# Mixing stage of a two-layer hybrid trunk: next pair's decay products and powers placed between this pair's corner products

## What is computed

```python
w_pre = rwkv_w0 + tanh(wl) @ rwkv_w2                    # decay product
decay = exp(-exp(-softplus(-w_pre) - 0.5))
a = sigmoid(rwkv_a0 + al @ rwkv_a2)
g = sigmoid(gl) @ rwkv_g2
kk = k * k_k; kk = kk * rsqrt(sum(kk * kk) + 1e-12)     # key norm
k_d = k * (1 + (a - 1) * k_a); b_d = kk * a
# scan over time, two directions:
S = S * w + (S @ -kk) b_d^T + v k_d^T ;  y = S r
bonus = sum(sum(r * k_d * r_k) * v)
```

## Time and profile before

| | before |
|---|---|
| median of 3 runs | 2956.99 us (2953.68 to 2960.45) |
| the profiled execution | 2950.64 us, span 2948.9 us |
| PE busy | 2860.9 us (97% of the span) |
| PEld, DVE, ACT busy | 58%, 43%, 25% |
| mean granted TensorE clock | 0.994 |
| mixing of layer 1, pairs | about 100 to 785 us of the span |
| mixing of layer 2, pairs | about 1860 to 2432 us of the span |

### The profile page before, as it was taken

One profiled execution on the slowest core, in us unless ns is written; L12 is line 12 of the kernel. 1 busy time (PEld: TensorE's weight loads), 2 busy tenths in 40 slices (PEclk: granted clock), 3 DMA queues, 4 the chain that ended last, 5 costly groups with the idle time before them and its releaser, 6 DMA issues.

```text
span 2948.9 us, 57155 instructions
## 1 busy us (share of the span) xinstructions
PE 2860.9 (97%) x25177; PEld 1721.3 (58%) x25177; DVE 1260.5 (43%) x2571; ACT 724.0 (25%) x1453; POOL 48.3 (2%) x76
## 2 busy tenths in 40 slices
PE   7999999999999999999999999999999999999999
PEld 3555555555654554444444444666666677788887
DVE  2566656555322221133333211566666643323551
ACT  3233333322222221011111001344333322211110
POOL 1000000000000000010000000000000000000000
PEclk9999999999999999999999999999999999999999
DMA  7111111111243333244444324212111124344554
GB/s 253 51 43 40 40 47 40 34 43 44 76 114 100 99 102 99 75 114 120 137 130 136 87 79 122 76 48 57 50 53 47 52 49 135 105 129 135 151 151 120
DMA packets 499989, 264.24 MB, mean 90 GB/s; under 512 B 42864, under 2 KB 493888, under 8 KB 499232
## 3 DMA queue, kind: packets, MB, share of 16 engines
q1 hardware_dynamic: 498016, 251.57, 29.9%
q0 software_dynamic: 1728, 9.03, 0.9%
HBM read 255.31 MB, written 5.24 MB: 88 GB/s over the span
## 4 chain that ended last, share of the span: by engine, by line
PE 90%; ACT 4%; DVE 4%; issue 1%; POOL 0%; DMA 0%; POOLq 0%; DVEq 0%; ACTq 0%
PE psum L453 56%; PE psum L1068 8%; PE psum L474 2%; PE psum L676 2%; PE psum L514 1%; PE psum L899 1%; PE psum L887 1%; ACT arena L1488 1%; PE psum L877 1%; PE psum L744 1%; PE psum L779 1%; PE psum L793 1%; PE psum L829 1%; PE psum L762 1%; PE psum L666 1%
## 5 line engine op out<-in xcount | busy, mean ns | idle before, releaser
L453 PE MATMUL psum<-hT,strips 128*128 128x512 f32 (+1 forms) x3968 | 1449.5, 512 | 4.0 <-ACT arena L1496 2.1
L453 PEld LDWEIGHTS psum<-hT,strips 128*128 128x128 f32 x3968 | 726.1, 190 | 504.2 <-issue 433.9
L1068 PE MATMUL psum<-arena,strips 128*128 128x512 f32 (+1 forms) x704 | 227.6, 486 | 0.6 <-DVE arena L2313 0.6
L1068 PEld LDWEIGHTS psum<-arena,strips 128*128 128x128 f32 x704 | 133.7, 190 | 93.5 <-issue 83.5
L453 PE MATMUL psum<-arena,strips 128*128 128x512 f32 (+1 forms) x512 | 167.9, 486 | 2.0 <-DVE done L2193 2.0
L1812 DVE TENSOR_SCALAR arena<-arena 128x512 f32<-128x512 f32 (+1 forms) x88 | 37.0, 420 | 278.9 <-ACT arena L1669 278.8
L1669 ACT COPY arena<-psum 128x512 f32<-128x512 f32 (+1 forms) x88 | 42.2, 480 | 412.2 <-PE psum L453 397.4
L453 PEld LDWEIGHTS psum<-arena,strips 128*128 128x128 f32 x512 | 97.1, 190 | 69.9 <-issue 60.7
L2159 DVE SCALAR_TENSOR_TENSOR arena<-arena,psum 128x512 f32<-128x512 f32 (+1 forms) x32 | 17.7, 554 | 268.1 <-PE psum L453 268.1
L2313 DVE SCALAR_TENSOR_TENSOR arena<-psum,mod,arena 128x256 f32<-128x256 f32 x24 | 10.9, 481 | 194.3 <-PE psum L1068 194.3
L1971 DVE TENSOR_TENSOR arena<-psum,tables 128x1024 f32<-128x1024 f32 x48 | 58.5, 1218 | 77.6 <-PE psum L676 77.6
(11 more groups left out here) (247 smaller groups left out, 3216.0 us busy)
## 6 DMA issues: line engine op xcount, KB each, us to landing
strips<-in_w_in_dram SPq DMA_DIRECT2D x158, 512.0 KB, 4.0
strips<-in_ffn_up_dram SPq DMA_DIRECT2D x88, 512.0 KB, 4.3
strips<-in_ada_w_dram SPq DMA_DIRECT2D x80, 512.0 KB, 4.1
strips<-in_ffn_down_dram SPq DMA_DIRECT2D x32, 512.0 KB, 4.0
arena<-in_ada_w_dram SPq DMA_DIRECT2D x4, 2048.0 KB, 14.6
strips<-in_w_in_dram SPq DMA_DIRECT2D x32, 256.0 KB, 3.8
strips<-in_a_out_w_dram SPq DMA_DIRECT2D x16, 512.0 KB, 4.1
strips<-in_rwkv_out_w_dram SPq DMA_DIRECT2D x16, 512.0 KB, 4.1
```

What stands on the lines that cost most here:

```text
L453: ins = mm(s.o[:, first:T], strip[:, b, k, :], rhs[:, k, first:T], k == 0, k == KT - 1)
L1068: ins = mm(s.o[:, lo:T], strip[:, b, j, :], hid[:, k, lo:T], k == 0, k == FT - 1)
```

## The change

The same work is done; its order inside the pair loop of `mix` changes on three engines, and two numbers of fill.

- PE: the bonus sums move from behind `corner_below` to behind the pair products `s10`, ahead of the corners. The second corner (`tr`) leaves `corners` and stands as `corners_right` behind `below_left`, just ahead of the value products. The next pair's two decay products move up: the first behind the pair products `s11`, the second ahead of `below_left`; the gate input `g` stays. The fill behind it becomes 2 units instead of 4 in layer 2, and `hop` there 2.15 instead of 2.
- ACT: the tanhs follow the copy of the first corner; the powers stand between the centre tap of k, the copy of `t10` and the key norm; the table loads move, one behind `head_inverse`, one ahead of the powers. Each tanh group now also waits for the bonus slot of this pair to be filled.
- DVE: `bonus` moves ahead of the mask of `s11`; `decays` and the first scan stand ahead of the copies of `x10`, the second scan behind them; four steps of the next pair's hats stand ahead of the chain over the chunks.

```diff
 # PE, pair loop
                     half_step(i)
                     pair_products(1, 0, i)
+                    bonus_sums(i)
                     fill(steps, 10 if wide or not ahead else 4)
                     corners(i)
                     pair_products(1, 1, i)
+                    if ahead:
+                        decay(0, i + 1)
                     fill(steps, 6 if wide or not ahead else 4)
+                    if ahead:
+                        decay(1, i + 1)
                     below_left(i)
+                    corners_right(i)
                     value_products(i)
                     fill(steps, 4 if wide or not ahead else 3)
                     corner_below(i)
-                    bonus_sums(i)
                     fill(steps, 4 if wide or not ahead else 5)
                     if ahead:
                         key_sums(i + 1)
-                        decays(i + 1)
-                        fill(steps, 4)
+                        gate_in(i + 1)
+                        fill(steps, 4 if wide else 2)
                     through_inverse(i, ahead)
-                    hop = (3.7 if ahead else 4) if wide else 2 if ahead else 2.3
+                    hop = (3.7 if ahead else 4) if wide else 2.15 if ahead else 2.3
 # ACT
+                def decay(q, i):
+                    if i > 0:
+                        act.wait_ge(*slots["bonus", l, i - 1].full)
+                    s = filled(f"decay{q}", i)
 ...
                     if i > 0:
                         head_inverse(i - 1)
+                        if ahead:
+                            exps_and_tanhs()
                     corners(i)
+                    if ahead:
+                        decay(0, i + 1)
+                        decay(1, i + 1)
+                    corners_right(i)
                     value_products(i)
                     if ahead:
                         centre(1, "k", i + 1, 0)
+                        logs()
+                        powers(0, i + 1)
                     else:
                         keys(1)
                     corner_below(i)
                     if ahead:
+                        powers(1, i + 1)
                         if lo:
                             conv_gate(i + 1)
                         key_norm(i + 1)
-                        decays(i + 1)
+                        gate_in(i + 1)
                     through_inverse(i)
                     if ahead:
                         if lo == 0:
                             conv_gate(i + 1)
-                        powers(0, i + 1)
-                        powers(1, i + 1)
 # DVE
+                    bonus(i)
                     masked_pairs(1, 1, i)
+                    if ahead:
+                        decays(i + 1)
+                        sums(0)
                     below_left(i)
                     if ahead:
+                        sums(1)
                         s = taps(1, "k", i + 1, 0, 1)
                         key_squares(i + 1, s)
-                    bonus(i)
                     state_in(0, i)
-                    if ahead:
-                        decays(i + 1)
                     steps = hats(i + 1) if ahead else iter(())
+                    for _ in range(EARLY_HATS):
+                        next(steps, None)
```

More of the change, by code:

```diff
@@ L621, in key_sums, with gate_in @@
                     one(s.o, tab["heads"], rinv_k).then_inc(s.full[0], 1)
[L623 to L629, removed]
+                def decay(q, i):
+                    if q == 0:
+                        pe.wait_ge(*lr.full())
+                    s = take(Q, f"decay{q}", l, i)
+                    for h in range(2):
+                        ins = one(PS[:, BANK_P[s.b] + h, :], lw[rows(h), q, :], low[rows(h), q, :])
+                    ins.then_inc(s.full[0], 1)
+                def gate_in(i):
                     s = take(A, "g", l, i)
@@ L705, in corners, with corners_right @@
                     ins.then_inc(s.full[0], 1)
+                def corners_right(i):
                     s = take(A, "tr", l, i)
@@ L991, in mix @@
                 pe.wait_ge(ev["low_ready"], l + 1)
-                decays(0)
+                decay(0, 0)
+                decay(1, 0)
+                gate_in(0)
                 pe.drain().then_inc(lr.free, 1)
@@ L1405, in key_norm @@
                 def key_norm(i):
-                    if i < 2:
+                    if i == 0:
                         logs()
@@ L1411, in key_norm, with decay, gate_in @@
                     act.activation(rinv_k, rinv_k, ACT.Exp, scale=-0.5).then_inc(ev["rinv_ready"], 1)
[L1412 to L1421, removed]
+                def decay(q, i):
+                    if i > 0:
+                        act.wait_ge(*slots["bonus", l, i - 1].full)
+                    s = filled(f"decay{q}", i)
+                    for d in range(2):
+                        o, v = seg2(PS[:, BANK_P[s.b] + d, :]), seg2(th[:, 2 * q + d, :])
+                        ins = act.activation(v[:, :, ::-1] if d else v, o, ACT.Tanh,
+                                             bias=pp[:, 19 + 2 * q + d, i:i + 1], scale=0.5)
+                    ins.then_inc(s.free, 1)
+                def gate_in(i):
                     s = filled("g", i)
@@ L1451, in head_inverse @@
                 def head_inverse(i):
-                    if i < KT - 1:
-                        logs()
                     s = filled("var", i)
@@ L1825, in conv @@
                     dve.wait_ge(*order.next())
+            EARLY_HATS = 4
             def mix(l, lo):
@@ L1887, in decays, with sums @@
                     dve.wait_ge(*t)
-                    for d in range(2):
-                        dve.tensor_tensor_scan(th[:, d, :], tab["restart"], th[:, d, :], 0.0, MUL, ADD)\
-                           .then_inc(ev["cum_ready"], 1)
+                def sums(d):
+                    dve.tensor_tensor_scan(th[:, d, :], tab["restart"], th[:, d, :], 0.0, MUL, ADD)\
+                       .then_inc(ev["cum_ready"], 1)
                 def hats(i):
```

## The result

The changed kernel takes 2929.91 us (median of 4 runs, 2928.23 to 2930.51), the kernel before, run beside it, 2955.34 us (4 runs, 2950.90 to 2960.45): ratio 0.9915 [0.9899, 0.9931], 25.4 us less. The forecast was 2948, with a range of 2940 to 2955: the sign was right, the gain nearly three times as large as forecast, and the time lies under the range.

The account below looks back on a forecast made before the run. PE's own work was taken to bound the kernel (busy 2860.9 of 2948.9 us). Terms -10.4 + 5.3 + 0.5 - 4.5 = -9.1 us gave 2948 against the median, range 2940 to 2955.

Parts of the forecast that it names:

- issue gaps: PE around the corners and pair products: waits for late instruction packets mostly go, 4.5 us stay; -10.4 us.
- bank of `tr`: Value products, all 16 pairs: `mv1` takes the bank of `tr` and waits about 0.33 us for ACT's copy; +5.3 us.
- ACT ahead of `through_inverse` and the chain: Layer 2: ACT's order before `through_inverse` costs +0.5 us, state products no longer waiting for DVE save 4.5 us.
- the clock: PE's granted clock: the prediction does not mention it and gave it no term.
- count of 256 instructions to a packet: PE's instruction queue: packets of 16.4 KB hold 252 records by calculation, 256 by the skill; PE stops where one ends.
- need of 3.6 us from one packet to the next: PE's instruction fetch: time from one packet's end to the next one's, taken from the gap at 2247.44.
- The rival that kept all gaps: PE's waits on "issue" stay as they are: +1.3 us, 2958, no measurable change; chance 0.12.
- the one that made them longer in the value products: Packet fetched in `below_left` comes 5.8 us late-style in 8 pairs, 3.1 us each: +13 us, 2970; chance 0.08.
- ACT ahead of `through_inverse`: Layer 2: wait for the copy of `g` goes (-4.7), waits for `conv_gate` (+3.2) and `lrb0` copies (+2.0) come; +0.5 us.
- The chain over the chunks: Layer 2 state products: early powers, four early hat steps and longer hops end waits for DVE; -4.5 us, bounds 0 and 5.2.
- More won: No gap stays in the new stretch and ACT reaches `conv_gate` in time: -16.8 us, 2940; chance 0.12.

Follow-up runs that it names:

- experiments 1: The kernel before with only the second corner (`tr`) moved behind `below_left` on PE and ACT: 2942.86 us, 0.9962 of the kernel before.
- experiment 2: The changed kernel with the second corner (`tr`) put back right behind the first on PE and ACT: 2940.71 us, 0.9960 of the kernel before.
- experiment 3: The kernel before with 64 idle wait instructions on PE at the start, shifting all later instructions in their packets: 2954.79 us, 1.0006 of the kernel before.
- experiment 4: The changed kernel with `conv_gate` ahead of the second group of powers on ACT in layer 2: 2924.82 us, 0.9900 of the kernel before.

## Why the prediction was wrong

Against the kernel before, in the account's terms (from the tables and experiments 1 and 2):

| term | forecast | measured |
|---|---|---|
| issue gaps | -10.4 | -13.5 |
| bank of `tr` | +5.3 | +3.9 |
| ACT ahead of `through_inverse` and the chain | -4.0 | -7.7 |
| the clock | none | -9.4 |

**The clock: the step that failed.** "What bounds each stretch is PE's own work, with gaps of 0.2 to 2 us": I priced a gap at its own length. The rows of before held the other part, six strips in 4.54 us at one place and in 2.84 at another, but I read one undisturbed pair and took its durations for all; and the list of waits cannot show the loss. It is more than a third of the gain, and more than half of the miss. The Trainium skill ("TensorE: Matmul & The Clock Gate", section "A second HAM failure mode: psum-queue depth-cycling") says that short idle times between groups of matmuls, if frequent, can make the clock swing between its two levels. The traces agree as far as that gaps of 1.2 to 2.1 us were followed by such stretches, at 1.7 us each, in 8 of 14 cases.

**The gaps: right in kind, too careful in size.** The count of 256 instructions to a packet held in every trace and in experiment 3, whose section shows the packets. In the region that I counted, the two traces of each kernel give -12.6 us; the other -0.9 is from the outputs. I left 2.0 us in four pairs of the first corner and 2.5 us in eight pairs of `below_left`; 1.4 us remained in that region in all (1.8 in the second trace). The output gaps stayed, 2.6 us. My need of 3.6 us from one packet to the next came from a single gap and lies near the top of what the kernel before shows, 3.1 us in the middle of its 18 gaps. Where a block of 256 begins in `below_left` in the changed kernel, the next one begins 2.1 to 3.4 us later, with no gap or one of at most 0.35 us. The rival that kept all gaps, and the one that made them longer in the value products, are refuted: the value products have 0.2 us, and 0.9 in the second trace.

**The bank of `tr`.** The wait is there. PE's timeline in a pair of layer 2 of the changed kernel, to be set against the earlier trace rows:

```profile
2037.39 1.15 PE L749 MATMUL psum<-arena 64*64 64x64 f32 x32
2038.73 1.15 PE L749 MATMUL psum<-arena 64*64 64x64 f32 x32 [0.19 <-ACT arena L1482]
...
2044.69 1.02 PE L621 MATMUL psum<-arena,tables 128*128 128x512 f32 x2
2045.55 0.59 PE L633 MATMUL psum<-low_rank,low_rank_out 128*128 128x256 f32 x2
2046.87 1.13 PE L453 MATMUL psum<-hT,strips 128*128 128x256 f32 x4 [0.72 <-ACT arena L1510]
2047.93 1.15 PE L767 MATMUL psum<-arena 64*64 64x64 f32 x32
2049.45 1.96 PE L767 MATMUL psum<-arena 64*64 64x128 f32 x32 [0.38 <-ACT arena L1502]
2051.35 0.45 PE L798 MATMUL psum<-arena 128*64 128x64 f32 x8
...
2059.40 0.45 PE L784 MATMUL psum<-arena 64*64 64x64 f32 x8
...
2062.27 0.45 PE L784 MATMUL psum<-arena 64*64 64x64 f32 x8
```

It shows 0.19 us where I had 0.33 (the rows that I named give 0.11 + 1.17 - 1.0 = 0.28). Start to start the value products take 2.41 us instead of 2.01; `tr` runs into the end of `below_left`, whose records stand between its own, and gives some of it back. Net it is 0.31 us in an undisturbed pair, with the second corner moved alone or last of all, 5.0 us over 16 pairs, and 3.9 by the account; why the two differ by 1.1 us isn't shown. The term was about right.

**ACT ahead of `through_inverse`.** ACT's rows of the same pair (the earlier trace rows before):

```profile
2039.92 0.58 ACT L1492 COPY arena<-psum 128x512 f32<-128x512 f32 x1 [0.64 <-PE psum L749]
...
2042.41 0.63 ACT L1447 ACTIVATE arena<-arena 128x512 f32<-128x512 f32 x1
...
2043.83 0.58 ACT L1486 COPY arena<-psum 32x512 f32<-32x512 f32 x1
...
2046.44 0.37 ACT L1510 COPY arena<-psum 128x256 f32<-128x256 f32 x1
```

`conv_gate` ends at 2046.81, 6.9 us after the copy of the second value slot began (2039.92); I had 6.6, with powers of 1.30 us a group, and they took 1.42 here (2042.41 to 2043.83). PE comes 6.3 us after the value products, as forecast, so the strip waits 0.72 us where I had 0.45. Start to start, key sums and gate input (with that wait behind it) take 2.18 us (2044.69 to 2046.87) instead of 1.49, +4.9 us over 7 pairs where +3.2 was forecast. `through_inverse` takes 3.42 us (2047.93 to 2051.35) instead of 3.78, in the first pair of layer 2 instead of 4.61: -3.4 (forecast -2.7). So this term is +1.5 instead of +0.5, and experiment 4 shows that the wait is real by taking it away.

**The chain over the chunks.** In layer 2 pairs whose strips no fall of the clock touches, all strips of a pair, each taken from its start to the next row's, take 31.21 us instead of 32.35: -1.14 us, 8.0 us over 7 pairs. The list of waits had shown 5.2 us, and I made that the upper bound. In such a pair the list shows 0.74 us of the 1.14; the rest does not stand there. A timeline of PE of the kernel before, three state products in a row:

```profile
2066.40 0.45 PE L779 MATMUL psum<-arena 64*64 64x64 f32 x8 [0.36 <-DVE arena L2088]
...
2069.64 0.45 PE L779 MATMUL psum<-arena 64*64 64x64 f32 x8 [0.20 <-DVE arena L2088]
...
2072.97 0.45 PE L779 MATMUL psum<-arena 64*64 64x64 f32 x8 [0.18 <-DVE arena L2088]
```

From one of these rows to the next it takes 3.24 us and 3.33 us; in the changed kernel the same work takes 2.87 (2059.40 to 2062.27 above). The excess is 0.83 us, and the brackets give 0.38. The list leaves out idle time of under 0.15 us. So 5.2 us was no upper bound. The two terms together are -8.0 + 1.5 = -6.5 by these pairs and -7.7 by experiment 2; the undisturbed pairs of layer 1 are 0.20 us shorter in experiment 2 than before (82.89 and 83.09), 1.6 over 8 pairs, which is of the size of the difference and which no term of mine had.

**Rivals and range.** "More won" (2940) came nearest, but by its own terms it holds only in part: few gaps are left, while ACT does not reach `conv_gate` in time. The lower end was the largest sum of the terms I had; a cost hanging on the gaps was outside of it by construction. What stays open is why one gap brings the clock down and a longer one doesn't.

## What to carry to other kernels

Before pricing a change by one clean stretch, compare the same instruction group in all places: one that takes 1.6 times as long somewhere points to the granted clock, and its loss stands under busy time. A short gap in dense small matmuls can cost its length and 1.7 us more, so closing gaps is worth more than their sum. And the total of a wait in the list can be far below what a late engine costs (here 5.2 of 8.0 us): take the bound from start-to-start times of undisturbed pairs.

## What was not expected of the hardware

Gaps of 0.2 to 2.35 us stand on PE at one place modulo 256 instructions, in every kernel here, and end 1.2 to 1.6 us behind the packet of instructions that they wait for; 64 more instructions in the prologue move them to other pairs at no change in time. A satisfied wait on PE costs some 0.05 us (48 of them, a gap of 2.32). A gap of 1.2 us or more among small products went with 3.4 us at 1.2 GHz, now and then 6.8, in 8 of 14 cases in the two traces of the kernel before. That also spreads the runs: the kernel before varied by 10 to 19 us from run to run (of 13 runs the shortest, 2945.01 us, had a mean granted clock of 0.996, the longest, 2963.69, of 0.990), the changed one by 2.3 in 4 runs.
